# Blocks 1 to 3: residual addition, squares, norm and turning of the rows each a pair or more apart

## The reference

```
xn   = RMSNorm(x);  proj = xn @ w_in
y_sb = stick-breaking attention of 8 heads x 64, strictly causal
y_ml = sigmoid(o) * HeadNorm(mLSTM of 4 heads x 128 in chunks)
mix  = (sigmoid(g_sb) * y_sb @ W_sb + sigmoid(g_ml) * y_ml @ W_ml) @ w_out
h    = x + mix
```

```
act = gelu(sum_d u[e, d] * hn[d]);   y += softmax gate * act * v[e, :]
out = RMSNorm(h + y)
```

## Time and profile before

| | |
|---|---|
| median of 3 runs | 3249.53 us (3244.43 to 3254.54) |
| the profiled execution | 3243.34 us; its span from first to last instruction 3241.2 us |
| busy: PE, DVE, ACT, POOL | 2583.2, 2073.1, 1127.0, 1204.6 us |
| moved by the DMA engines | 1259.44 MB, of which gathers 1073.81 MB |
| first gather issued, last pair begun | 274.91 us, 3228.24 us |

### The profile page before, as it was taken

The page is one execution under the profiler, slowest core; times in us unless marked ns, Lnnn a source line. Parts: engine busy times, 40 slices in busy tenths (PEclk is TensorE's granted clock), DMA queues, the critical chain, the costliest instruction groups (busy, mean ns, idle before and its releaser), DMA issues.

```text
span 3241.2 us, 40454 instructions
## 1 busy us (share of the span) xinstructions
PE 2583.2 (80%) x14564; PEld 1312.7 (41%) x14564; DVE 2073.1 (64%) x4803; ACT 1127.0 (35%) x3546; POOL 1204.6 (37%) x1048
## 2 busy tenths in 40 slices
PE   8998988998898788997887777998787555555555
PEld 6776544555364244553454233455353111111111
DVE  2324769777458888764448898775447857765454
ACT  2212345342323653332323473334222332232222
POOL 0002334333334453343334465333333444444443
PEclk9999999999999899999898999999898777777777
DMA  4465999999999999999999999999999999999997
GB/s 155 134 193 231 411 414 395 414 418 417 397 414 418 410 421 417 417 418 418 416 414 397 416 403 420 416 418 417 417 415 414 406 422 421 418 419 417 419 421 329
DMA packets 220328, 1259.44 MB, mean 389 GB/s; under 512 B 24289, under 2 KB 28385, under 8 KB 89057
## 3 DMA queue, kind: packets, MB, share of 16 engines
q0 software_dynamic: 147456, 1073.81, 80.3%
q1 hardware_dynamic: 65168, 162.61, 13.6%
q10 hardware_dynamic: 7504, 20.45, 1.6%
HBM read 1251.01 MB, written 5.77 MB: 388 GB/s over the span
## 4 chain that ended last, share of the span: by engine, by line
DMA 40%; PE 35%; DVE 9%; issue 6%; ACT 6%; POOL 3%; SPq 0%; DVEq 0%; POOLq 0%; ACTq 0%
DMA rowsb<-uv,e_idx 37%; PE yacc L991 13%; PE mixp L631 8%; DVE rowsb L1849 4%; POOL rowsb L1064 3%; PE mixp L656 3%; DMA wt<-w_query_ 2%; PE mixp L730 2%; ACT diag L1383 2%; ACT wg L1378 2%; PE mixp L643 1%; PE yacc L631 1%; DVE area L1493 1%; PE mixp L668 1%; ACT gmt L1364 1%
## 5 line engine op out<-in xcount | busy, mean ns | idle before, releaser
L1064 POOL DMA_INDIRECT rowsb<-uv,e_idx x1024 | 1200.4, 1172 | 2011.2 <-PE yacc L991 1575.0
L1849 DVE CUSTOM_DVE_ANT_0 rowsb<-rowsb,hnrow 128x1024 f32<-128x1024 f32 x1024 | 1242.1, 1223 | 835.9 <-DMA rowsb<-uv,e_idx 834.1
L991 PE MATMUL yacc<-rowsb,diag 64*64 64x512 f32 x8192 | 1192.3, 705 | 604.3 <-ACT diag L1383 590.3
L991 PEld LDWEIGHTS yacc<-rowsb,diag 64*64 64x64 f32 x8192 | 294.0, 148 | 1329.5 <-ACT diag L1383 907.5
L1364 ACT ACTIVATE gmt<-dots 128x2 f32<-128x2 f32 x512 | 104.1, 203 | 1564.0 <-DVE dots L1849 1563.2
L631 PE MATMUL mixp<-area,wt 128*128 128x256 f32 x2112 | 489.4, 386 | 1.3 <-DMA wt<-w_feat 1.3
L631 PEld LDWEIGHTS mixp<-area,wt 128*128 128x128 f32 x2112 | 393.9, 191 | 130.6 <-issue 80.7
L1383 ACT ACTIVATE diag<-ident,wg 128x64 f32<-128x64 f32 x1024 | 300.3, 340 | 16.7
L1378 ACT ACTIVATE wg<-gmt,gate 128x1 f32<-128x1 f32 x1024 | 245.5, 286 | 17.7
L656 PE MATMUL mixp<-area,wt 128*128 128x256 f32 x960 | 226.7, 390 | 6.8 <-DMA wt<-w_query_ 6.3
L1082 ACT ACTIVATE area<-mixp 128x512 f32<-128x512 f32 (+3 forms) x314 | 136.6, 481 | 268.3 <-PE mixp L631 151.4
(11 more groups left out here) (263 smaller groups left out, 1823.4 us busy)
## 6 DMA issues: line engine op xcount, KB each, us to landing
wt<-w_merge SPq DMA_DIRECT2D x96, 512.0 KB, 8.2
wt<-w_feat SPq DMA_DIRECT2D x80, 512.0 KB, 7.9
wt<-w_query_ SPq DMA_DIRECT2D x62, 512.0 KB, 12.1
wt<-w_tok SPq DMA_DIRECT2D x32, 512.0 KB, 11.0
rowsb<-uv,e_idx POOLq DMA_INDIRECT x1024, 13.1
wt<-w_out_ SPq DMA_DIRECT2D x24, 512.0 KB, 8.4
rowsb<-w_out_ SPq DMA_DIRECT2D x8, 512.0 KB, 4.6
area<-keysT ACTq DMA_DIRECT2D x16, 256.0 KB, 8.2
```

What stands on the lines that cost most here:

```text
L991: last = pe.matmul(yacc[at:at + HP, k % 2, c * NCH:(c + 1) * NCH], diag[r * HP:(r + 1) * HP, s, :], rowsb[r * HP:(r + 1) * HP, s, D + c * ...
L1064: pool.indirect_dma_start(rowsb[:, n % RS, :], None, uv, bass.IndirectOffsetOnAxis(ap=e_idx[:, i % 2, k:k + 1], axis=0)).then_inc(row_load ...
L1849: dve.tensor_tensor_reduce(rowsb[:, s, 0:D], rowsb[:, s, 0:D], hnrow[:, i % HR, :], 1.0, 0.0, ALU.mult, ALU.add, dots[:, s:s + 1]).then_in ...
```

## The change

`N_OUT` goes from 9 to 10 and `N_HN` from 3 to 5. Between the last unit of the output product and the addition of the input stands an empty step; the squares and the root stay in the first step of the norm, DVE's normed rows are in the third, TensorE's turning in the fourth and ACT's copies in the fifth. The planner's costs follow. And the allowance of two steps a pair in block 1 ends 26 steps before the block's end, which is with the output product's last unit; from there it is one.

```diff
@@ -381,7 +381,7 @@
 
         N_NORM, N_PROJ1, N_PROJ2 = 3, len(PROJ1) + 1, len(PROJ2) + 1
         AT_ROWS, AT_BML = 4 * ML_HEADS + 1, len(BULK)
-        N_MIX, N_OUT, N_HN, N_QRY = len(BULK) + 5, KD + 1, 3, len(QRY) + 3
+        N_MIX, N_OUT, N_HN, N_QRY = len(BULK) + 5, KD + 2, 5, len(QRY) + 3
 
         UNIT_PE, UNIT_DMA, PART_DVE = 3.3, 1.25, 1.75
 
@@ -418,8 +418,8 @@
                     dve_ += 1.7
                 pe_ = UNIT_PE + (0.9 if h < ML_HEADS else 0.2) if k < AT_BML + 4 else 0.2
                 load.append((pe_, dve_, UNIT_DMA if k < AT_BML + 4 else 0.0))
-            load += [(UNIT_PE, 0.0, UNIT_DMA)] * KD + [(0.0, 2.8, 0.0)]
-            load += [(1.0, 0.0, 1.25), (2.9, 2.7, 0.0), (1.0, 0.0, 2.5)]
+            load += [(UNIT_PE, 0.0, UNIT_DMA)] * KD + [(1.0, 0.0, 0.0), (0.0, 2.8, 0.0)]
+            load += [(1.0, 0.0, 1.25), (1.0, 0.0, 0.0), (0.0, 2.7, 0.0), (2.9, 0.0, 0.0), (1.0, 0.0, 2.5)]
             load += [(UNIT_PE + 0.3, 0.0, UNIT_DMA + 0.2)] * len(QRY) + [(1.0, 0.0, 0.6)] * 3
             return load
 
@@ -467,7 +467,7 @@
                 behind = [max(0.0, q) + r - e for q, r, e in zip(behind, slot_load(s), (min(each, max(6.4, each - 1.0)), each - 0.8, each))]
                 while k < len(cost[b]) and (s % PP > 1 or s < PP):
                     small = max(cost[b][k][:2]) < 0.9
-                    if count[s] == (2 if b == 1 else 1) and not small:
+                    if count[s] == (2 if b == 1 and k < len(cost[b]) - N_QRY - N_HN - 2 else 1) and not small:
                         break
                     after = [q + r for q, r in zip(behind, cost[b][k])]
                     if max(after) > 2.0 and not (even and count[s] == 0):
@@ -943,7 +943,7 @@
 
 
                     for k in range(N_HN if b > 0 else 0):
-                        if k == 1:
+                        if k == 3:
                             for t in range(NT):
                                 turn_rows(b, t)
                         yield
@@ -1314,7 +1314,7 @@
                                                   ).then_inc(h_stored[t0 + t], 16)
                                 act.wait_ge(dot_done, (t0 - 1) * NSEL)
                                 square_row(t)
-                            if k == 2:
+                            if k == 4:
                                 for c in range(2):
                                     keep_turned(t, c)
                         if k == 0:
@@ -1710,7 +1710,7 @@
                                                 ).then_inc(x_taken[bank(key)], 1)
                             yield
                     for k in range(N_OUT if b > 0 else 0):
-                        if k == KD:
+                        if k == KD + 1:
                             dve.wait_ge(xrow_loaded[0], 16 * (b + 1))
                             if b < 2:
                                 dve.wait_ge(xrow_loaded[1], 16 * (b + 1))
@@ -1719,7 +1719,7 @@
                                 add_input(n)
                         yield
                     for k in range(N_HN if b > 0 else 0):
-                        if k == 1:
+                        if k == 2:
                             dve.wait_ge(std_ready, b + 2)
                             mark(dve.reciprocal(ssq[:, 0:NT], ssq[:, NT:2 * NT]))
                             dve.wait_ge(nrow_loaded, 16 * (b + 1))

```

## The result

The changed kernel takes 3282.76 us in the median of 4 runs (3279.39 to 3286.93), the kernel before 3250.49 beside it (4 runs): 1.0105 times as long, 95% interval 1.0092 to 1.0117. It is slower by some 34 us by the ratio, where +13.6 had been forecast, and lies outside the range. The profiled execution took 3281.85 us, its span is 3279.7: 38.5 more than before.

The account below looks back on a forecast made before the run. Bound by bytes over the DMA rate (417 GB/s) plus idle time when the pile, up to eight gathers asked for and not landed, runs dry. Terms sum to +13.6 us on 3243.3, giving 3256.9, as median 3263; range 3248 to 3277.

Parts of the forecast that it names:

- A: Block 1's proj1, pairs 14 to 24: packed into 8 pairs instead of 11, length 57.9 us, idle time +0.5 us.
- E: Block 1's output, norm and queries, pairs 82 to 107: 4.6 us of idle time before the change.
- the norm chain: Block 1, 860 to 880 us: setting the norm's links apart regains all the DMA time lost there, -2.4 us.
- B: Block 1's attention, pairs 25 to 36: 9 pairs instead of 12, length 63.3 us, pile empty, +12 us (7 to 14).
- C: Block 1's proj2, pairs 37 to 49: 10 pairs instead of 13, length 66.7 to 71.2 us, idle time +1.5 us.
- D: Block 1's merge, pairs 50 to 81: 30 pairs, TensorE's 187.7 us balanced with 186 of bytes except at its start, +1.5 us.
- Block 3's +0.5: Block 3's attention packed by two pairs: 0 to +4 us, taken with block 2's later queries as +0.5 us together.
- Rival 3: Starving spreads from block 1's attention through proj2 and merge, the pile staying empty: +28 us, median 3278; chance 0.06.
- Rival 1: The pile carries more, or DVE's first wait in B shrinks: about +5 us, median 3255; chance 0.23.
- rival 2: Packing is free, as TensorE and DVE have spare time in A and B: medians 3239 to 3247; chance 0.07.
- Rival 4: At the norm, DVE's late rows are held by the choice of experts, 2.4 us stay: +16 us, median 3266; chance 0.03.
- Rival 5: In B, POOL's gather issues wait 0.6 us in the mean for DVE's dot products: +11 on top, median 3274; chance 0.03.

Follow-up runs that it names:

- e2: Kernel before, with block 1's proj1 and attention packed as in the changed kernel (pairs 14 to 30), proj2 onward as before: ratio 1.0031 to before.
- e6: Kernel before, with only block 1's proj2 packed into 10 pairs (37 to 46), attention and merge as before: ratio 1.0032.
- e8: Changed kernel with gathers of 4 KB a row instead of 8, every instruction and wait kept: 2903.4 us, one execution.
- e10: Kernel before, proj2 in the same 10 pairs (37 to 46), but first six steps one a pair, last eight two a pair: ratio 1.0005.
- e9: Kernel before with gathers of 4 KB a row instead of 8: 2874.11 us, one execution.
- e4: Changed kernel with block 1 wholly as before, so only blocks 2 and 3 changed: ratio 1.0006 to before.
- e7: Kernel before, with only block 1's norm links set a pair apart from pair 88 on, last queries sharing pairs: ratio 0.9999.
- e11: Kernel before, with block 1's attention in 14 pairs instead of 12, merge in 31 instead of 32, norm links apart: ratio 0.9978, median 3243.54 us.
- e12: Kernel before, with block 1's attention in 14 pairs, merge in 31, but norm links together as before: ratio 0.9997.
- e3: Kernel before, with block 1's proj1, attention and proj2 packed as in the changed kernel, merge and the rest as before: ratio 1.0069.

## Why the prediction was wrong

**What held.** The direction; the rate, which is still 415 to 417 GB/s where the engines are kept busy (A, E, block 2); the norm chain in size: by the GB/s the dip had 3.4 us of idle time and has 1.2, -2.2 for a forecast of -2.4. (The 2.4 was read from the share; by the rule used for every other term the whole dip was 3.4.) B's idle time too, +11.0 for +12, but there two errors cancel, which is luck: B takes 73.4 us and not 63.3, A 47.2 and not 57.9. TensorE ends A two units behind (260 matmuls there, where three pairs less would be 292), and DVE's first wait in B is 14.5 us instead of 7.1. A and B together take 120.6 us, forecast 121.2. In the 47.2 us of A 19.6 MB are moved and 22.5 asked for, so B finds a pile where the prediction had none. e2 confirms the sum of A and B within its interval (10 us, 6 to 15). Of the signs that I had named, the fallen share in B and the smaller dip came. Two did not come: DVE is busy 73% of B and not over 80%, since it waits for TensorE, and in A it still waits 14.7 us for rows, in ten waits, where I had expected none to speak of.

**What failed: the length of C.** The step was "the pairs' time on the bound engine" comes off a stretch's length: 77.1 - 5.9 at most, 66.7 to 71.2 us, and +1.5 idle. It is 81.1, and +12.6. A pair taken away takes off TensorE's 1.95 us only if the waits stay as they are. Here second steps came into pairs whose first step feeds them, DVE stood 6 us longer at each of L1526 and L1551, and the dot products behind it came late, with them ACT and TensorE. The 8.3 us at L1834 come from proj2's last steps meeting the choice of experts in one pair, which the prediction had not looked at either. e6 shows it with the pile filled, e8 with half the bytes, and e10 takes it away by the order of the steps alone. Its 71.7 us lie just above the estimate's upper end, 71.2: the estimate was one of a packing without those waits, at the full clock.

**What failed: "balanced" for D.** I took TensorE's 187.7 us for D's length and compared it with the bytes. TensorE's busy time came out so (189.0), but the length is 200.5. The earlier trace rows gave no warning because the bytes covered it: the engines' own length was 196.8 before (e9) under 205.1 of bytes. Taking away two pairs' bytes uncovered it, packing added to it (200.3 in e8), and C left no pile to pay from. That the waits for L896 are what makes it longer is read from the waits; no run takes them away. Idle +16.8 in the profile; from the ratios, about 10 us of the loss.

**The rest.** Block 3's +0.5 was costed at two pairs of attention; neither e4 (1.0006) nor the profile shows more than its own grain.

**The rivals.** Rival 3, starving that spreads, came nearest in time, 3278 as median, and had 0.06. Its mechanism is half right: D's loss does grow behind an emptied pile, but C's arises in C. Rival 1 is out, idle time in B rose by 11 us; rival 2 is out with it. Rival 4 is out: the dip at the norm is down to 1.2 us, and in e7 to 0.3 in the pairs where it was 3.3.

Rival 5 is right in its mechanism and wrong in its price. The changed kernel in B (POOL, then DVE):

```profile
434.96 0.94 POOL L1064 DMA_INDIRECT rowsb<-uv,e_idx  x1 [7.55 <-PE yacc L991]
...
474.20 1.97 POOL L1064 DMA_INDIRECT rowsb<-uv,e_idx  x1 [0.30 <-issue]
```

```profile
474.14 1.22 DVE L1849 CUSTOM_DVE_ANT_0 rowsb<-rowsb,hnrow 128x1024 f32<-128x1024 f32 x1
```

At 434.96 us DVE stands still, and the issue takes 0.94 us. At 474.20 one begins just behind the start of a dot product that ends at 475.36, and it ends 0.81 us after that. Counted over the changed kernel: 370 issues begin while DVE does nothing and take 0.93 to 0.95 us. 454 begin within a dot product and take 1.41 in the mean. 225 of these begin with over 0.6 us of it to go; they take 1.71 in the mean, and 212 of them end between 0.80 and 0.82 us after it. The 15 that begin within L1818, 0.69 us of DVE with one input, take 0.93 to 0.94; the 19 within L1811, as long but with two inputs, 1.07 in the mean and up to 1.45. The mean of 1.17 hid this, and the prediction's "not yet a whole blocked instruction" was read from means. The Trainium skill's rule, "SBUF — State Buffer", section "SBUF: two separate sides", says that of a DVE instruction with two on-chip inputs and a GpSimd one the later is blocked for the other's whole instruction, and this trace bears it out one way: an issue that begins within such a DVE instruction is held until it ends. The other way it does not show, for the 367 dot products that begin during an issue take 1.22 us like the rest. The loss doesn't come from this: the 20 issues in the packed attention take 23.10 us, 4.4 more than at 0.94 each, where the 24 before took 8.6 more, and POOL waits 47.0 us for TensorE there.

## What to carry to other kernels

Before steps are moved closer, ask for each engine that works its program in order which of its waits land in the same slot as the work they wait for; a stretch's length is not the busy time of its bound engine less what was moved out. A stretch covered by its bytes hides how long its engines need; running it with half the bytes shows that length directly. When a prefetched stream starves, give slots to the stretches whose engines take longer than their bytes, and take them where bytes bind; here that paid in e11, together with the spacing, and not to be seen in e12, without it. And a mean over a thousand instructions can hide two kinds of them: look at single ones before calling a rule not borne out.

## What the hardware showed that I had not expected

TensorE's granted clock was lower in the packed proj2: 1.00 in the mean before and 0.95 now, and the pair's product at its start took 3.59 us instead of 1.95. TensorE was busy 70.1 us in C, against 66.6 in e10, whose clock stayed at 1.00, for as many matmuls: up to 3.5 us of C's length are the clock, 1.6 of them at that place. It looks as if it followed the starved attention (TensorE busy 58.5 us of 73.4 at a clock of 0.93), but the runs do not show that. In e2 the attention is packed in the same way and two products behind it (32 records) take 3.80 us together; in e6 the attention is the one of before, and the first product takes 3.52. These two lines are e2's and e6's:

```profile
506.79 3.80 PE L991 MATMUL yacc<-rowsb,diag 64*64 64x512 f32 x32 [1.59 <-ACT diag L1383]
```

```profile
524.56 3.52 PE L991 MATMUL yacc<-rowsb,diag 64*64 64x512 f32 x16 [1.81 <-ACT diag L1383]
```

The slow product is there in the four kernels with the changed kernel's proj2 packing (the changed one, e3, e6, e8) and in none of the others, yet it stands ahead of proj2's first step. What lowers the clock there stays open.

Windows view of the changed kernel at that product and behind it:

```profile
503.00:505.00 2.00, 1.93 (x12) 0.74 (x16) 0.00 (x0) 0.01 (x1) 0.00 (x0) 0.56 0.97 352
505.00:507.00 2.00, 2.00 (x10) 0.27 (x3) 0.00 (x0) 0.00 (x0) 0.06 (x1) 0.59 0.63 254
507.00:509.00 2.00, 2.00 (x11) 1.02 (x9) 0.00 (x0) 0.00 (x0) 1.70 (x2) 1.00 0.34 74
```
